# Two blocks of a transformer on one core: plain rows turned at two stage ends, and the order of the put-back matmuls

## What is computed

```python
x = x + g_a * _merge(ya, yb, ga, gb, w_oa[l], w_ob[l], w_out[l])
hx = _modulate(_rmsnorm(x, norm_mlp[l]), sh_m, sc_m)
x = x + g_m * moe(hx.reshape(b * s, d)).reshape(b, s, d)
```

```python
def rmsnorm(x, g):
    xf = x.astype(F32)
    y = xf * lax.rsqrt(jnp.mean(xf * xf, axis=-1, keepdims=True) + EPS)
    return (y * g.astype(F32)).astype(x.dtype)

for layer in range(DEPTH_2):
    u = rmsnorm(h, norm_mix[layer])
    y = mlstm_mixer(u, ...) if layer == 0 else moba_mixer(u, positions, ...)
    h = h + y
    h = h + swiglu(rmsnorm(h, norm_ffn[layer]), ffn_w_in[layer], ffn_w_out[layer])
```

## Time and profile before

| | us |
|---|---|
| runs | 1852.09, 1844.4, 1844.58 |
| median | 1844.58 |
| span of the profiled execution | 1850.4 |
| TensorE busy | 1767.8 |
| DVE busy | 790.0 |
| ACT busy | 573.5 |
| the 31 put-backs from the first to the one before the last | 364.83 to 1221.66 |
| last put-back, start | 1233.33 |

### The profile page before, as it was taken

The page is one execution under the profiler, slowest core; times in us unless marked ns, Lnnn a source line. Parts: engine busy times, 40 slices in busy tenths (PEclk is TensorE's granted clock), DMA queues, the critical chain, the costliest instruction groups (busy, mean ns, idle before and its releaser), DMA issues.

```text
span 1850.4 us, 22797 instructions
## 1 busy us (share of the span) xinstructions
PE 1767.8 (96%) x9358; PEld 1044.6 (56%) x9358; DVE 790.0 (43%) x1423; ACT 573.5 (31%) x1036; POOL 22.2 (1%) x59
## 2 busy tenths in 40 slices
PE   5989999999999999999999999989999999999999
PEld 4978787333333333333232323338788887888887
DVE  2887964111111111111111111125577776767776
ACT  4446563001001001001010110125554445664443
POOL 1020010000000000000000000000000000000000
PEclk9999998999999999999999999999999999999999
DMA  8655477999999999999999999995445636335551
GB/s 312 228 195 183 146 296 293 385 426 428 426 427 427 427 427 427 426 428 427 427 427 427 427 427 426 427 376 183 137 137 179 227 118 244 137 119 166 198 184 44
DMA packets 122045, 563.10 MB, mean 304 GB/s; under 512 B 7216, under 2 KB 53424, under 8 KB 97360
## 3 DMA queue, kind: packets, MB, share of 16 engines
q1 hardware_dynamic: 121104, 558.70, 75.9%
q10 hardware_dynamic: 832, 2.89, 0.4%
HBM read 560.52 MB, written 1.05 MB: 303 GB/s over the span
## 4 chain that ended last, share of the span: by engine, by line
PE 74%; DMA 19%; DVE 4%; ACT 2%; issue 1%; SPq 0%; ACTq 0%; DVEq 0%
PE ps L1112 15%; PE ps L1135 10%; DMA arena<-in_w_up 9%; PE ps L1390 9%; PE ps L666 7%; PE ps L667 7%; PE ps L668 7%; DMA ring<-in_w_up 7%; PE ps L1391 4%; PE ps L1050 2%; PE ps L1070 2%; DMA ring<-in_w_ada 1%; DVE part L2079 1%; PE ps L991 1%; DMA ring<-in_w_in 1%
## 5 line engine op out<-in xcount | busy, mean ns | idle before, releaser
L2079 DVE TENSOR_TENSOR part<-ring,part 128x1024 fp32r<-128x1024 f32 (+2 forms) x299 | 320.5, 1091 | 142.9 <-ACT part L1517 142.5
L666 PE MATMUL ps<-part,part 128*128 128x512 f32 (+1 forms) x888 | 313.7, 353 | 7.4 <-DVE part L2079 3.9
L667 PE MATMUL ps<-part,part 128*128 128x512 f32 (+1 forms) x888 | 302.8, 341 | 0.0
L668 PE MATMUL ps<-part,part 128*128 128x512 f32 (+1 forms) x888 | 302.6, 341 | 0.0
L1517 ACT ACTIVATE part<-ring 128x1024 fp32r<-128x1024 f32 (+2 forms) x299 | 272.3, 945 | 90.9 <-DVE ring L2079 69.6
L1112 PE MATMUL ps<-ring,arena 128*64 128x512 f32 x1216 | 269.9, 595 | 10.5 <-DMA ring<-in_w_up 10.3
L1390 PE MATMUL ps<-part,part 128*128 128x512 f32 x704 | 250.3, 398 | 0.0
L2076 DVE TENSOR_SCALAR arena<-ps 128x512 f32<-128x512 f32 x64 | 44.3, 692 | 428.3 <-PE ps L1112 428.3
L1391 PE MATMUL ps<-part,part 128*128 128x256 f32 x704 | 197.4, 280 | 0.0
L1112 PEld LDWEIGHTS ps<-ring,arena 128*64 128x64 f32 x1216 | 84.1, 137 | 193.3 <-issue 169.1
L666 PEld LDWEIGHTS ps<-part,part 128*128 128x128 f32 x888 | 169.2, 191 | 36.6 <-issue 8.7
(11 more groups left out here) (274 smaller groups left out, 1477.2 us busy)
## 6 DMA issues: line engine op xcount, KB each, us to landing
ring<-in_w_down SPq DMA_DIRECT2D x39, 2048.0 KB, 35.1
ring<-in_w_up SPq DMA_DIRECT2D x38, 2048.0 KB, 35.5
ring<-in_w_gate SPq DMA_DIRECT2D x38, 2048.0 KB, 34.6
arena<-in_w_up SPq DMA_DIRECT2D x26, 2048.0 KB, 36.5
ring<-in_ffn_w_in SPq DMA_DIRECT2D x44, 1024.0 KB, 8.0
arena<-in_w_down SPq DMA_DIRECT2D x18, 2048.0 KB, 36.6
spare<-in_w_gate SPq DMA_DIRECT2D x13, 2048.0 KB, 34.9
arena<-in_w_gate SPq DMA_DIRECT2D x13, 2048.0 KB, 34.2
```

The costliest lines, as they stand in the source:

```text
L666: e.matmul(out, x[0], y[0], start=first, stop=False, skip_group_check=True)
L667: e.matmul(out, x[0], y[1], start=False, stop=False, skip_group_check=True)
L668: return e.matmul(out, x[1], y[0], start=False, stop=last, skip_group_check=True)
L2079: return e.tensor_tensor(out, x, y, op)
```

## The change

The changed kernel does three things.

At "moe", plain rows are turned by transposes, both token halves of a k into one PSUM bank (`turn_both`), and evicted together: 8 evictions of 256 columns on ACT and 8 on DVE in place of 16 and 16 of 128 columns. Turnings k = 0 to 3 stand ahead of the first product, 4 to 7 between its steps. The weight low of that product's piece is made in two halves (`first_low`). Squares, sum and root come behind the evictions. The root then scales v (as its square, r2), the sigmoid's input, the gate columns (together with their bias, now a parameter of 8 columns in all partitions), the ones column of v and the floor of the denominator's norm. The root is taken by Ln and Exp in place of Sqrt and a reciprocal, and one table load on ACT goes. TensorE's turning of the gate rows waits for a copy ("rows") that now stands on DVE behind `low(C0 + 3)`.

At "ffn0", the same is done as at "e": plain transposes in pairs between the final products, where the places are those of "e", the last four behind the first part of the MoBA in-projection. The root scales v's evictions and the eps of q's and k's norms.

In `put_back` the loop order is changed to h outer, q inner (`moe_rows`), for all experts; `rows_update` follows the same order at "moe".

```diff
+        moe_rows = [(q, h) for h in range(2) for q in range(2)]
...
+            def turn_both(k):
+
+                if k % 4 == 0:
+                    for q in range(2):
+                        e.wait_ge(*s_xn.of("moe", q, k // 4))
+                if k >= 4:
+                    e.wait_ge(*s_ulo.of("c", k - 4))
+                for q in range(2):
+                    i = e.transpose(PS[turned_bank("moe", k)][:, 128 * q:128 * q + 128], X[:, q, 128 * k:128 * k + 128], C("ident"))
+                i.then_inc(*s_ut.up("c", k))
...
-                    for q in range(2):
-                        for h in range(2):
-                            i = e.matmul(b.Y[q][h], b.PwT[ex % 2][CAP * h:CAP * h + CAP, 128 * q:128 * q + 128],
-                                         b.yg[CAP * h:CAP * h + CAP, :], start=False, stop=ex == NE - 1,
-                                         skip_group_check=True)
+                    for q, h in moe_rows:
+                        i = e.matmul(b.Y[q][h], b.PwT[ex % 2][CAP * h:CAP * h + CAP, 128 * q:128 * q + 128],
+                                     b.yg[CAP * h:CAP * h + CAP, :], start=False, stop=ex == NE - 1,
+                                     skip_group_check=True)
...
+                     "ffn0": {(1, 0, 1): 0, (1, 0, 2): 2, (1, 0, 3): 4, (1, 1, 0): 6, (1, 1, 2): 8, (1, 1, 3): 10},
...
-                    if (q, h) == (1, 1) and x % 2 == 0 and stage == "ffn0":
-                        turn_rows(stage, *range(2 * x, 2 * x + 4))
...
-                    for k in range(8):
+                    for k in range(2):
                         e.wait_ge(*s_ulo.of("e", k))
                     e.wait_ge(*s_xn.of("ffn0", 0, 0))
                     slab("b_in", m_slabs[0], 4, 0, (0,))
-                    turn_rows(stage, *range(8, 12))
+                    turn_rows(stage, *range(12, 16))
...
-            turn_rows("moe", *both_halves[0:4])
+            for k in range(4):
+                turn_both(k)
...
                 if j == 1:
-                    e.wait_ge(*s_cg.of("bias"))
+                    e.wait_ge(*s_cg.of("rows"))
...
+                if stage == "moe":
+                    for k in range(8):
+                        e.wait_ge(*s_ut.of("c", k))
+                        e.activation(up[:, 0, k, :], PS[turned_bank("moe", k)][:, 0:T], ACT.Copy, scale=P(gain[0], 8 * gain[1] + k)
+                                     ).then_inc(*s_uhi.up("c", k))
+                    for q, h in moe_rows[1:]:
+                        squares_of(q, h)
+                    high(C0 + 2)
+                    root_of(0)
+                    root_of(1)
+                    return
...
-                        copy(c.v[:, q, 2 * s:2 * s + 2, 0:T], PS[2 * s + q].rearrange("p (h n) -> p h n", h=2)).then_inc(*s_cev.up("v", s, q))
+                        e.wait_ge(*s_factor.of("square", q))
+                        e.activation(c.v[:, q, 2 * s:2 * s + 2, 0:T], PS[2 * s + q].rearrange("p (h n) -> p h n", h=2), ACT.Copy, scale=c.r2[q]
+                                     ).then_inc(*s_cev.up("v", s, q))
...
+                    rows_update(stage, 1, 0)
+                    first_low(0)
+                    rows_update(stage, 0, 1)
+                    pair_low(0)
+                    pair_low(1)
+                    rows_update(stage, 1, 1)
+                    pair_low(2)
+                    pair_low(3)
+                    first_low(1)
+                    for k in range(4, 8):
+                        pair_low(k)
+                    return
...
-                    ts(c.gT, PS[5][0:8, 0:T], P("bgates", p=8), None, ALU.add).then_inc(*s_cg.up("bias"))
+                    e.tensor_copy(c.gT, PS[5][0:8, 0:T]).then_inc(*s_cg.up("rows"))
```

More of the change, by code:

```diff
@@ L479, in build @@
         c.den = [tiny(4) for _ in range(8)]
+        c.r, c.r2, c.floor = ([tiny(1) for _ in range(2)] for _ in range(3))
+        s_factor = signal("row_factors")
         s_wghi, s_wglo = signal("gate_weights_high"), signal("gate_weights_low")
@@ L607, in turned_bank @@
         def turned_bank(stage, i):
-            return ends[stage][2] + (2 * (i % 8) + i // 8 if stage == "moe" else i) % 4
-        both_halves = [8 * q + k for k in range(8) for q in range(2)]
+            return ends[stage][2] + i % 4
+        moe_rows = [(q, h) for h in range(2) for q in range(2)]
         def score_at(h):
@@ L1765, in turned_high @@
                                  scale=P(gain[0], 8 * gain[1] + k)).then_inc(*s_uhi.up(to, i))
-                if stage in ("c", "e"):
+                if stage in ("c", "ffn0", "e"):
                     for g in range(4):
@@ L2009, in m_root @@
                     e.wait_ge(*s_mvec.of("squares", i, q))
-                e.activation(m.rr[i], m.ss[i], ACT.Ln, bias=C("eps", 1) if d else C("eps128", 1), scale=1.0 / 128 if d else 1.0
-                             ).then_inc(*s_mrr.up("ln", i))
-                e.wait_ge(*s_mrr.of("ln", i))
+                    e.wait_ge(*s_factor.of("m", q))
+                    part = slice(4 * q, 4 * q + 4)
+                    e.activation(m.rr[i][:, part], m.ss[i][:, part], ACT.Ln, bias=(m.eps_k if d else m.eps_q)[q], scale=1.0 / 128 if d else 1.0
+                                 ).then_inc(*s_mrr.up("ln", i, q))
+                for q in range(2):
+                    e.wait_ge(*s_mrr.of("ln", i, q))
                 e.activation(m.rr[i], m.rr[i], ACT.Exp, scale=-0.5).then_inc(*s_mrr.up(i))
@@ L2359, in next_norm @@
                             turned_low(i)
-                        if g == 2:
+                        if g == 2 and stage != "ffn0":
                             diagonal(0)
+                    if stage == "ffn0":
+                        low(E0 + 2)
+                        for q in range(2):
+                            diagonal(q)
+                        for q in range(2):
+                            e.wait_ge(*s_xss.of(stage, q))
+                            total = xstat[q][:, 2:3]
+                            ts(m.eps_k[q], total, EPS / D, EPS * EPS, ALU.mult, ALU.add)
+                            ts(m.eps_q[q], total, 128 * EPS / D, 128 * EPS * EPS, ALU.mult, ALU.add).then_inc(*s_factor.up("m", q))
+                        return
                     diagonal(1)
```

160 lines of the change are left out of this document (79 added, 81 removed).

## The result

The changed kernel takes 1825.72 us, the median of 6 runs (1824.96 to 1832.55), against 1845.1 us of the kernel before (1844.2 to 1852.23), also of 6. That is 19.4 us less. The ratio is 0.9888 (the two medians alone give 0.9895), with a 95% interval of 0.987 to 0.9905. The prediction was 1840.9, with a range from 1830.5 to 1845 and "no change that can be measured" as the likeliest verdict.

What follows compares the result with a forecast made beforehand. TensorE, busy 96% of the span, was taken as the bound, with DMA limiting the late expert loop. On the median 1844.58, -12.95 for the two stage ends and +9.2 for the put-backs gave 1840.9 us, range 1830.5 to 1845.

Steps and rivals of the forecast that it cites:

- Part 3: Put-backs of all 32 experts: the new order costs +.85 us per expert, +2.6 on the profiled execution, +9.2 on the median.
- if matmuls start strictly in order: Put-backs: the second matmul waits, the third joins it, the fourth waits; 3 slots, 2.84 us instead of 1.99.
- Rival B: Put-backs: the new order costs nothing, since matmuls for free rows pass the waiting one; 1831.6 us, 22%.
- A: The forecast itself, put-backs dearer by .85 us per expert: 1841, own range 1834.5 to 1844; 50%.
- The cover: Expert loop: DMA sets the late pace, so 23.1 us hide TensorE work that is added per expert.
- 6.6 of the 7.5 us: Median against profiled execution, 7.5 us below: 6.6 placed in the DMA-bound stretch, the rest in loads at the start.
- Part 1: Experts' end: no diagonal, fewer evictions; 8.5 us saved, .65 lost to a new wait: -7.85 us (-9 to -5).
- The walk on DVE: Experts' end: DVE's chain stepped through from the last put-back's start; last product out 8.95 us after it, now 17.45.
- turning needs only the updated rows: Experts' end: with the diagonal gone, first transposes start 2.8 us after the last put-back's start; earlier turning saves 3.5 us.
- case E: Experts' end: TensorE's clock falls again, on top of A: 1843.4 us, 5%.
- The new wait of .65: Experts' end: TensorE's turning of the gate rows waits for their copy on DVE; .65 us lost, 0 to 1.5.
- Part 2: End of ffn0: plain transposes woven between final products, three waits gone: -5.1 us (-5.7 to -3.5).

Runs made afterwards that it cites:

- before_small_tiles: Kernel before, 8 unused columns behind par and 24 just ahead of the ring, so X and small tiles move by 32 bytes, the ring by 128: 1847.75 us, ratio 0.9991.
- after_old_order: Changed kernel with the put-backs of experts 0 to 30 in the order of before, the last in the new order: 1831.17 us, ratio 0.99.
- before_shift32: Kernel before with one unused tile of 32 bytes behind par, moving every later tile, the ring to 26880: 1840.71 us, ratio 0.9945.
- after_no_dense: Changed kernel without the untaken branch (computation for all tokens) on TensorE, so no jump behind the last put-back: 1827.53 us, ratio 0.9881.
- the experiment: Changed kernel with the end of ffn0 as before (diagonal products, no weaving): 1836.46 us, ratio 0.9945.
- after_swapped: Changed kernel with TensorE's two branches exchanged, which moves the jump ahead of the expert loop: 1832.57 us, ratio 0.9923.
- after_tail: Changed kernel with all that TensorE does behind the experts written into both branches, so the taken one doesn't jump: 1828.48 us, ratio 0.9876.

## Why the prediction was wrong, point by point

The forecast was -12.95 for the two stage ends and +9.2 for the put-backs. The profiles show -9.4 and 0, and -10.3 for which the sum had no term.

- **Part 3, the put-backs: the step failed.** I priced a pair on the same rows at one slot more, .85, from L1011, where all matmuls share a row group. The price of a same-row pair is right, since the two do run one after the other. What failed is "if matmuls start strictly in order". The two row halves are served side by side, each in its own order. Two matmuls for each half are two slots, however they are interleaved: 1.99. Rival B, which I gave 22%, has the mechanism. The Trainium skill, "TensorE: Matmul & The Clock Gate", Part 3, "What overlaps and what doesn't", says that matmuls keep program order in start and end. By that rule I leaned to A. The starts in the changed kernel's trace (13 ns, against 1 us for the one that stands ahead) do not agree with it for matmuls on different rows; the order of the semaphore increments (P+1.13, 1.99, 2.04, 2.08) does.
- **The cover.** The 23.1 us by which DMA covers TensorE's work in the loop was read rightly, but it was never drawn on. That 6.6 of the 7.5 us between the executions lie in the DMA's part was a guess, and wrong. In the traces the loop takes 861.3 to 862.7 us whenever the ring is at 26880, however the whole ran. The difference lies ahead of the loop. The nearest case is before_small_tiles, the kernel before but for padding that did nothing: its profiled span is 8.4 us below that of before, and 7.7 of these are there by the first put-back (357.1 against 364.8), 0.8 in the loop. The granted clock goes with it: in the window from 312 to 322 us it is 0.55 in the profile of before, 0.66 after and 1.00 in before_small_tiles and after_old_order. The first view is of before, the second of after_old_order:

```profile
312.00:322.00 10.00, 10.00 (x43) 7.42 (x44) 1.29 (x6) 2.52 (x4) 0.00 (x0) 0.55 0.39 164
```

```profile
312.00:322.00 10.00, 10.00 (x50) 3.35 (x48) 0.32 (x2) 1.35 (x2) 0.00 (x0) 1.00 0.60 216
```

- **Part 1: -7.85 forecast, -4.2 measured.** The walk on DVE was right: without the jump the first transposes came at P+2.85 (2.8 forecast) and the gate products at P+9.09 (8.95). The failed step is "turning needs only the updated rows". TensorE also needs its next instructions. The idle 4.34 us of the earlier trace rows, put down to DVE's diagonal, had a second cause behind the first: the diagonal was ready at P+5.83, but TensorE went on at P+6.33, while in before_shift32, with the diagonal ready at the same P+5.83, it went on at P+5.89. The changed kernels that have the jump and no diagonal there start at P+6.10 to 6.42. So removing the diagonal could win next to nothing of the first turning. The clock, too, fell again (0.64), which I had as case E at 5%. The new wait of .65 didn't show: in after_no_dense the gate rows' copy started at P+14.33, not 15.3, and the turning, at P+14.86, was not held up.
- **Part 2: -5.1 forecast, -5.2 by the traces and by the experiment.** Right in mechanism and size. Of the waits that stayed the longest is .4, twice the .20 that stage e had shown and within the .6 that was forecast.
- **What no term of the sum held: 10 us from the ring's address.** I treated the 8 columns of bgates as a parameter's size only, and the DMA's 29.4 us per expert as a fixed line. I had even said that 1 us on that line is 1 us of the result, but had no reason for it to move. In the loop it gave 6.2 us; ahead of it, the first product that waits for the loads came 2.1 us earlier (42.10 against 44.23). The first put-back's 4.1 us hold what is left of these 2.1 and what the clock did there in this execution; how they share it isn't settled, so of the 10 us the 6.2 of the loop are read from the traces. The medians of whole runs fit a gain of about 10: the ratio of the kernel before is 0.9942 to 0.9947 with the ring moved to 26880 and 0.9985 and 0.9991 with the paddings that left it 96 bytes past a multiple of 128.
- **The verdict.** Parts 1 and 2 as they came, 9.4 us, with B's zero for part 3 would have given 1835.7: just faster than by .5%. The range missed because its low end lay 1.1 us below B's own centre, with nothing left for what no case held. Rival B had the mechanism of the put-backs, and its centre, 1831.6, is the nearest of all to the 1825.72 measured, but that is in part luck: B took both stage ends at 12.95, and the 10 us of the ring made up for more than they fell short.

## What to carry to other kernels

A change in the size of one tile moves all the tiles behind it: where the kernel hangs on loads, compare the addresses of the loads' target tiles before and after, and try some paddings of up to 256 bytes, since each costs one line. An idle time that ends with the last of several conditions says nothing about the others; before you price its removal, ask what else would have to be ready, and behind a long jump that includes the instructions. Code behind a branch with one usual side can stand inside both sides, so that the usual side doesn't jump.

## What the runs showed of the hardware that I had not expected

- Loads of 16 KB packets ran at 430 GB/s with the base of the ring at 26880, and at 427 or 428 with it 32, 64 or 96 bytes past a multiple of 128 (a packet 612.4 ns against 616.1 to 616.7 on average); at 27008, a multiple of 128 but not of 256, it was 429 and 613.9. The Trainium skill, "DMA: Bandwidth & Descriptors", "How a descriptor splits into AXI transactions", has transfers split at multiples of 256 bytes, and one that starts off such a multiple pay for more. The direction agrees. Its count, in which the bytes ahead of the start cost, would have 224 past a multiple of 256 (26848) dearer than 32 past one (26912), and these are alike here; and the arena's slots paid nothing at 96 past a multiple of 128. Why the arena is exempt stays open.
- A jump of TensorE over more than 5000 instructions left it idle for 4.13 us at the end of the experts, where it would have waited 0.86 without, and the gate products came 4.2 us later by it; ahead of the experts the idle time was 6.34 us. An instruction load of 16 KB stands in both gaps: at P+3.45 (0.88 us), and TensorE goes on 1.8 us after its end; at 310.16 (0.94 us) in after_swapped, and TensorE goes on 1.6 us after its end. In after_no_dense and after_tail none of this size starts between P and P+10. With the ring off 26880 TensorE goes on at P+6.26 or later, with it there at P+6.10 to 6.18 in the changed kernels.
- Matmuls on rows 0 to 63 and on rows 64 to 127 pass one another: each half of the rows is served in its own order (starts 13 ns apart for the first and the third of the program). Their semaphore increments still come in the order of the program (P+1.13, 1.99, 2.04, 2.08).
